# Value projections of a hybrid decoder block: 512 weight columns a matmul instead of 256

## What is computed

```
h = rmsnorm(x);  proj = h @ w_in          # w_in: 2048 x IN_COLS
nq, nkv, ngate, rq, rk, rv, rg, mq, bg = split(proj)
# nkv: (k_c, v_c, k_s, v_s, k_w, v_w), each 2 groups x 128 = 256 columns
# sparse attention: o = g0*softmax(q k_c')v_c' + g1*softmax(q k_s)v_s + g2*softmax(q k_w)v_w
#   k_c', v_c' = silu(blocks(k_c) @ cmp_w1) @ cmp_w2, and the same for v_c
# retention: 4 heads, rq, rk 128 columns each, rv 4 x 256 = 1024 columns
```

## Time and profile before

| | |
|---|---|
| median of 3 runs | 1707.71 us |
| profiled execution, its span from first to last instruction | 1705.8 us |
| PE busy | 1696.5 us (99%) |
| PE weight loads busy | 1468.2 us (86%) |
| DVE busy | 1132.7 us (66%) |
| ACT busy | 827.3 us (49%) |
| mean share of the 16 DMA engines on the main queue | 61.3% |
| DMA share in the v_s slot (251.2 to 266.6 us) | 0.88 |
| granted TensorE clock, mean | 0.999 |

### The profile page before, as it was taken

How to read it: one execution, slowest core, us unless ns; L and a number is a source line. 1 busy time by engine, 2 the same in 40 slices (tenths; PEclk the granted TensorE clock), 3 DMA queues, 4 the chain that set the end, 5 groups by cost and what they waited for, 6 DMA issues and landing times.

```text
span 1705.8 us, 25366 instructions
## 1 busy us (share of the span) xinstructions
PE 1696.5 (99%) x9082; PEld 1468.2 (86%) x9082; DVE 1132.7 (66%) x1522; ACT 827.3 (49%) x1139; POOL 48.0 (3%) x53
## 2 busy tenths in 40 slices
PE   9999999999999999999999999999999999999998
PEld 8888899999888888888888888888888888888886
DVE  7755676667475554554565777777776776776777
ACT  7544455444444444444444755455454555454453
POOL 1000000000140000000000000000000000000000
PEclk9999999999999999999999999999999999999999
DMA  9666478345656666666557566665666666656654
GB/s 304 189 230 198 138 232 260 118 142 159 202 158 185 197 190 194 212 195 196 188 186 242 177 188 197 193 199 185 195 190 189 186 192 189 190 191 192 193 176 148
DMA packets 245992, 327.78 MB, mean 192 GB/s; under 512 B 12907, under 2 KB 167308, under 8 KB 245388
## 3 DMA queue, kind: packets, MB, share of 16 engines
q1 hardware_dynamic: 245900, 326.47, 61.3%
HBM read 321.71 MB, written 3.67 MB: 191 GB/s over the span
## 4 chain that ended last, share of the span: by engine, by line
PE 98%; issue 1%; DVE 0%; DMA 0%; ACT 0%; POOL 0%; POOLq 0%; DVEq 0%; ACTq 0%
PE bank L1481 19%; PE bank L1471 15%; PE bank L1473 15%; PE bank L1472 15%; PE bank L1485 10%; PE bank L1494 7%; PE bank L1499 4%; PE bank L1458 1%; PE bank L1460 1%; PE bank L1459 1%; PE bank L1445 1%; PE bank L1447 1%; PE bank L1446 1%; PE bank L1766 0%; PE bank L1767 0%
## 5 line engine op out<-in xcount | busy, mean ns | idle before, releaser
L904 DVE TENSOR_TENSOR wlo<-wraw,whi 128x1024 fp32r<-128x1024 f32 x584 | 714.9, 1233 | 400.3 <-ACT whi L593 398.0
L593 ACT ACTIVATE whi<-wraw 128x1024 fp32r<-128x1024 f32 x584 | 616.7, 1059 | 625.2 <-PE bank L1473 378.7
L1481 PE MATMUL bank<-hx,whi 128*128 128x512 f32 x1376 | 344.5, 392 | 0.0
L1481 PEld LDWEIGHTS bank<-hx,whi 128*128 128x128 f32 x1376 | 248.0, 189 | 44.7
L1485 PEld LDWEIGHTS bank<-hx,wlo 128*128 128x128 f32 x1376 | 187.7, 190 | 13.4
L1485 PE MATMUL bank<-hx,wlo 128*128 128x256 f32 x1376 | 191.9, 282 | 0.0
L1471 PE MATMUL bank<-whi,hx 128*128 128x512 f32 x448 | 175.7, 392 | 0.0
L1473 PE MATMUL bank<-whi,hx 128*128 128x512 f32 x448 | 174.4, 389 | 0.0
L1472 PE MATMUL bank<-wlo,hx 128*128 128x512 f32 x448 | 174.3, 389 | 0.0
L1471 PE MATMUL bank<-whi,r_hi 128*128 128x512 f32 x384 | 149.8, 390 | 0.0
L1472 PE MATMUL bank<-wlo,r_hi 128*128 128x512 f32 x384 | 149.5, 389 | 0.0
(11 more groups left out here) (272 smaller groups left out, 2039.2 us busy)
## 6 DMA issues: line engine op xcount, KB each, us to landing
wraw<-in_w_in SPq DMA_DIRECT2D x200, 512.0 KB, 3.7
wraw<-in_w_up SPq DMA_DIRECT2D x176, 512.0 KB, 4.5
wraw<-in_w_down SPq DMA_DIRECT2D x88, 512.0 KB, 3.8
wraw<-in_w_mem_kv SPq DMA_DIRECT2D x32, 512.0 KB, 4.5
wraw<-in_w_o SPq DMA_DIRECT2D x32, 512.0 KB, 4.4
wraw<-in_w_br_mem SPq DMA_DIRECT2D x16, 512.0 KB, 4.4
wraw<-in_w_br_nsa SPq DMA_DIRECT2D x16, 512.0 KB, 4.3
wraw<-in_w_br_ret SPq DMA_DIRECT2D x16, 512.0 KB, 4.0
```

The lines of the kernel that those rows point to most:

```text
L593: nc.scalar.activation(whi[:, c], wraw[:, c], ACT.Copy).then_inc(hi_done, 1)
L904: V.tensor_tensor(wlo[:, c], wraw[:, c], whi[:, c].bitcast(F32), ALU.subtract).then_inc(lo_done, 1)
L1481: T.matmul(ps[UP_PAIRS[j][t]][:, :], whi[:, c, k, t * P:(t + 1) * P], hx[:, :, k0 + k, :], start=first and k == 0, stop=False, skip_group_ ...
```

## The change

- **Retention values.** The four quads of "rv" become two groups of two quads, each with 512 weight columns and 16 feature tiles. They use `chunk_w` (12 matmuls of 512 columns) in place of `chunk_n`. A group lives in two banks (0 and 7, then 1 and 0), and is read out once, by two DVE instructions of 128x512 at the end of its second quad. The loop over them is written out on PE and DVE.
- **Sparse values.** v_s and v_w are computed together: a matmul streams 256 columns of v_s from one buffer and 256 of v_w from another, 512 in all (`values_pair`). In quads 5 and 6, chunk 0 holds v_s and chunk 2 v_w of the same 4 feature tiles, and PE does both in 24 matmuls of 512 before the two compression chunks. In quad 9, chunks 0 and 1 are one pair and chunks 2 and 3 the next. `hidden` and `compressed` come in the middle of the two pairs. The sums stay in banks 1 and 4 from quad 5 to the end of quad 9, and are read out once.
- **Counting.** `values_pair` waits for the later of its two chunks and counts `pe_done` once it is through: in quads 5 and 6 by 1 after the pair and by 2 after the compression chunk 1; in quad 9 by 2 after each pair.
- The number of bytes loaded, of splits and of products is the same.

```diff
-          ("rqk", 4, 4), ("rv", 4, 4), ("rg", 4, 2),
+          ("rqk", 4, 4), ("rv", 4, 2), ("rg", 4, 2),
+RV_PAIRS = ((0, 7), (1, 0))
+VV_PAIR = (1, 4)
...
 # SP
-                         rows(w_in, 4 * (2 * h + c // 2), at))
-            quad(Q0["mix"] + 9, lambda c: rows(w_in, 4 * c, C_KV + 5 * GW))
-
-            loop(Q0["rqk"], 4, 2, cols(w_in, C_RQ))
+                         rows(w_in, 4 * h, C_KV + (3 + c) * GW) if n == 3 else rows(w_in, 4 * (2 * h + c // 2), at))
+            quad(Q0["mix"] + 9, lambda c: rows(w_in, 8 + 4 * (c // 2), (C_KV + 3 * GW, C_KV + 5 * GW)[c % 2]))
+
+            loop(Q0["rqk"], 2, 2, cols(w_in, C_RQ))
+            loop(Q0["rv"], 2, 2, wide_cols(w_in, C_RV), into_wide)
...
 # DVE
-                elif n == 3:
-                    by_row(q + 1, b, arena[:, A_VS:A_VS + 512], (), (), 3)
-                else:
+                elif n != 3:
...
-            by_row(q, 1, arena[:, A_VW:A_VW + 512], ())
+            dve.wait_ge(pe_done, 4 * q + 4)
+            for t in range(TT):
+                ch.add(V.tensor_scalar(arena[:, A_VS:A_VS + 2 * (A_VW - A_VS)].rearrange("p (a t n) -> p a t n", a=2, n=S)[:, :, t, :],
+                                       ps[VV_PAIR[t]][:, :].rearrange("p (a n) -> p a n", a=2), rstd_col(0, t), None, ALU.mult))
+            ch.wait()
+
+            dve.sem_inc(evac[1], 2)
+            ahead(q, (3,))
...
-                            by_row(q, j, arena[:, bass.ds(1024 * i + (base + 512 * j), 512)], ())
+                            if j:
+                                dve.wait_ge(pe_done, 4 * q + 4)
+                                for t in range(TT):
+                                    ch.add(V.tensor_scalar(by_head(A_RV + 1024 * i, t), ps[RV_PAIRS[i][t]][:, :].rearrange("p (h n) -> p h n", h=2),
+                                                           rstd_col(0, t), None, ALU.mult))
+                                ch.wait()
+                                dve.sem_inc(evac[i], 1)
+                            ahead(q, (3,))
...
 # PE
+            def values_pair(q, a, b, k0, first, last, between=None):
+
+                pe.wait_ge(lo_done, 4 * q + b + 1)
+                for t in range(TT):
+                    o = ps[VV_PAIR[t]][:, :]
+                    for k in range(CK):
+                        xh, xl = (v[:, k0 + k, t * P:(t + 1) * P] for v in (h_hi, h_lo))
+                        vh, vl = (v[:, a:b + 1:b - a, k, :] for v in (whi, wlo))
+                        T.matmul(o, xh, vh, start=first and k == 0, stop=False)
+                        T.matmul(o, xh, vl, start=False, stop=False)
+                        e = T.matmul(o, xl, vh, start=False, stop=last and k == CK - 1)
+                    if t == 0 and between is not None:
+                        between()
+                return e
...
-                    if n == 3:
-                        chunk_n(*at, b, *H, 4 * i, i == 0, i == 3)
-                    else:
+                    if n != 3:
                         chunk_d(*at, KEY_PAIRS[b], hx, 4 * i, i == 0, i == 3)
-                    compress_chunk(at[0], at[1] + 1, m, i)
-            quad(chunk_n, Q0["mix"] + 9, 1, (g + 5) // 2, H, {0: hidden, 2: compressed})
+                    elif i % 2 == 0:
+                        values_pair(at[0], 0, 2, 2 * i, i == 0, False).then_inc(pe_done, 1)
+                    compress_chunk(at[0], at[1] + 1, m, i, 2 if n == 3 and i % 2 == 0 else 1)
+            values_pair(Q0["mix"] + 9, 0, 1, 8, False, False, hidden).then_inc(pe_done, 2)
+            values_pair(Q0["mix"] + 9, 2, 3, 12, False, True, compressed).then_inc(pe_done, 2)
...
+            for i in range(2):
+                for j in range(2):
+                    scores, transposes, output = sparse(1, j, 2 * i + (HPG + j))
+                    scores()
+                    if j == 0:
+
+                        pe.wait_ge(evac[i], G0["rv"] // 2)
+                        if i:
+                            pe.wait_ge(evac[0], G0["rv"] // 2 + 1)
+                    for c in range(4):
+                        chunk_w(Q0["rv"] + 2 * i + j, c, RV_PAIRS[i], *H, 8 * j + 2 * c, j == 0 and c == 0, j == 1 and c == 3)
+                        if c == NSA_BEFORE[-1]:
+                            transposes()
+                    output()
```

More of the change, by code:

```diff
@@ L1105, in _, with sparse_softmax @@
                             ALU.mult).then_inc(s_kce, 1)
-            by_row(q, 1, arena[:, A_VW:A_VW + 512], ())
+            dve.wait_ge(pe_done, 4 * q + 4)
[5 more added lines that the diff above has]
+            ahead(q, (3,))
             dve.wait_ge(s_tab, 16)
             dve.wait_ge(s_sig, 1)
[L1111 to L1115, removed]
+            def sparse_softmax(g, i, j, h, q):
                         dve.wait_ge(a_s, h + 2)
@@ L1146, in _ @@
                         if g == 0:
-                            by_column(q, j, arena[:, bass.ds(1024 * i + (base + 512 * j), 512)], chunks=())
+                            by_column(q, j, arena[:, bass.ds(1024 * i + (A_RQ + 512 * j), 512)], chunks=())
                         else:
-                            by_row(q, j, arena[:, bass.ds(1024 * i + (base + 512 * j), 512)], ())
+                            if j:
[6 more added lines that the diff above has]
+                            ahead(q, (3,))
                         dve.wait_ge(a_h, h + 1)
@@ L1152, in _ @@
                                         ALU.subtract).then_inc(a_l, 1)
-                    ch.leave(2, NSA_LINKS * 2)
+            with dve.Fori(0, 2) as i:
+                ch.enter(i, NSA_LINKS * 2)
+                for j in range(2):
+                    sparse_softmax(0, i, j, 2 * i + j, 2 * i + (Q0["rqk"] + j))
+                ch.leave(2, NSA_LINKS * 2)
+            for i in range(2):
+                for j in range(2):
+                    sparse_softmax(1, i, j, 2 * i + (HPG + j), 2 * i + (Q0["rv"] + j))
             for i in range(2):
@@ L1756, in compressed, with compress_chunk @@
                 e.then_inc(s_kc, 1)
-            def compress_chunk(q, c, m, n):
+            def values_pair(q, a, b, k0, first, last, between=None):
[11 more added lines that the diff above has]
+                return e
+            def compress_chunk(q, c, m, n, done):
                 pe.wait_ge(s_bkl, m // 2 + 1)
@@ L1767, in compress_chunk @@
                     e = T.matmul(o, x_, wlo[:, c, k, :], start=False, stop=m % 2 == 1 and n == 3 and k == CK - 1)
-                e.then_inc(pe_done, 1)
+                e.then_inc(pe_done, done)
             g = G0["mix"]
@@ L1776, in _, with sparse @@
                     at = (q + i // 2, 2 * (i % 2))
-                    if n == 3:
-                        chunk_n(*at, b, *H, 4 * i, i == 0, i == 3)
-                    else:
+                    if n != 3:
                         chunk_d(*at, KEY_PAIRS[b], hx, 4 * i, i == 0, i == 3)
-                    compress_chunk(at[0], at[1] + 1, m, i)
-            quad(chunk_n, Q0["mix"] + 9, 1, (g + 5) // 2, H, {0: hidden, 2: compressed})
[L1785 to L1788, removed]
+                    elif i % 2 == 0:
[3 more added lines that the diff above has]
+            values_pair(Q0["mix"] + 9, 2, 3, 12, False, True, compressed).then_inc(pe_done, 2)
+            def sparse(g, j, h):
                         def scores():
@@ L1824, in output @@
                                      skip_group_check=True).then_inc(a_o, 1)
-                        quad((chunk_t, chunk_n)[g], q, j, i + G0[ph] // 2, H, {-1: scores, NSA_BEFORE[-1]: transposes, 3: output})
+                        return scores, transposes, output
+            with pe.Fori(0, 2) as i:
+                for j in range(2):
+                    scores, transposes, output = sparse(0, j, 2 * i + j)
+                    quad(chunk_t, 2 * i + (Q0["rqk"] + j), j, i + G0["rqk"] // 2, H, {-1: scores, NSA_BEFORE[-1]: transposes, 3: output})
+            for i in range(2):
+                for j in range(2):
+                    scores, transposes, output = sparse(1, j, 2 * i + (HPG + j))
[9 more added lines that the diff above has]
+                    output()
             octets("rg", H)
```

## The result

The changed kernel took 1718.25 us (median of 4 runs, 1716.53 to 1720.16), the kernel before 1707.6 us in the same comparison. The ratio is 1.0063, with a 95% interval of 1.0051 to 1.0075: 10.6 us slower. Forecast were 1715.5 us, a range of 1709.5 to 1719, and slower with a chance of 0.91.

The account below looks back on a forecast made before the run. PE's instruction stream was taken to bound the kernel. Waits of 3.84 + 3.2 + 3.1 and small terms of 0.4 make 10.5 us, less 2.7 for the stream: +7.8, so 1715.5 us; range for 8 in 10, 1709.5 to 1719.

Parts of the forecast that it names:

- signs that I had named for being wrong: In the trace after: PE starting the pair at once, a clock slice under 1.0, or a pair costing 0.24 us a matmul or more.
- Bound by PE's stream, waits not recovered: Whole kernel: PE is 99% busy, so any wait of PE lengthens the kernel by the full wait.
- Entry of quad 5: Before quad 5's pair: PE waits from 251.22 to 255.06 for the split of chunk (5, 2), +3.84 us.
- Quad 5 to quad 6: Before quad 6's pair: PE waits for rounding and three splits after the late release, +3.2 us (3.0 with overlapping splits, else 3.4).
- End of quad 9: Before head 0's scores: buffer 2 is released only when the last pair ends, so PE waits for `vc`, +3.1 us.
- Quad 9's start: Before quad 9's first pair: PE waits for the split of chunk (9, 1), +0.2 us.
- Stream: Fewer, wider matmuls: -1.7 us in "rv" after restart losses and -1.0 in "mix", together -2.7 us.
- "Hidden" work: Softmax, copies and read-out of two 512-column banks run beside other work and cost nothing.
- The clock: Rival: clock falls in PE's pauses, 2.6 us each; 1718.1 us after one fall, 1723.3 after three; chance 0.12. Forecast sum: nothing.

Follow-up runs that it names:

- e8: e3 with head 0's softmax maxima ahead of split 2 and the v_s/v_w read-out on DVE, split 3 after the probabilities: 1711.95 us.
- e6: e5 with quads 5 and 6 using chunks that hold both v_s and v_w, only quad 9 paired over two buffers, filling before head 0's scores: 1708.1 us.
- e5: Changed kernel plus ten spare 512-column matmuls before quad 5's pair, quad 6's pair and head 0's scores (the filled kernel): 1715.09 us.
- e1: Kernel before with only the retention values changed to 512 columns, sparse values as before: 1705.33 us.
- e3: e5 without the filling before head 0's scores, DVE making `kc` and `vc` before split 2 of the next quad: 1714.02 us.
- e2: Kernel before with only the sparse values paired, retention values as before: 1720.99 us.
- e7: e5 with each product of a pair done in two 256-column matmuls, one a buffer: 1715.24 us.
- e9: Changed kernel with v_s and v_w in one chunk in quads 5 and 6, quad 9 paired over two buffers, DVE's order of e8, no filling: 1705.48 us.

## Why the prediction was right, step by step

The mechanism and the sign were right, the total too small by 2.8 us. One of the signs that I had named for being wrong did appear: a slice of the clock under 1.0 (0.83 from 250 to 260 us), and with it a pair at 7.16 / 24 = 0.30 us a matmul. So the forecast's term for the clock, nothing, failed.

- **Bound by PE's stream, waits not recovered.** Right: each wait taken away came back in the total (e8: 1.8 expected, 2.1 measured; e6: 6.8 and 7.0, though its term for quad 9 is not borne out).
- **Entry of quad 5, +3.84.** 2.74 in the profile after, 3.0 in e5. The kind was right. The size was read from one execution in which the chain came late: DVE's read-out of quad 4 began at 252.34 there and at 251.11 after, 1.2 us earlier, with the same order of work up to that point. The trace of e1, whose mix phase is that of the kernel before, confirms it. Its rows (PE at the start of quad 5, then DVE's read-out of quad 4 and split (5, 2)):

```profile
250.97 0.28 PE L1473 MATMUL bank<-whi,hx 128*128 128x256 f32 x1
...
250.97 0.75 DVE L926 TENSOR_TENSOR arena<-bank,arena 128x256 f32<-128x256 f32 x2
...
252.63 1.23 DVE L907 TENSOR_TENSOR wlo<-wraw,whi 128x1024 fp32r<-128x1024 f32 x1 [0.18 <-ACT whi L596]
```

  There the split ended at 253.86, 2.9 us after PE came to the quad.
- **Quad 5 to quad 6, +3.2.** 2.99; the four splits took 4.63 us, so they overlap by 0.1 each, the lower of the two bounds.
- **End of quad 9, +3.1.** 3.14. But as a repair the step was incomplete: I named the read-out as "queued on DVE behind `vc`" with "only split 3" behind it. The head's softmax stands there as well, which e3 showed, once the wait ahead of it was gone.
- **Quad 9's start, +0.2.** 1.4: the term that was mis-sized most. I took the distance of split (9, 1) from PE as fixed. It was not: the data came late (ACT waited 1.51 us for them). Why they did stays open. With quads 5 and 6 as changed, the wait is 1.2 us in the trace after, 1.3 in e2, 1.0 in e5 and e8, 1.5 in e3 and none in e7. With their buffers released one by one it is 0.9 in e6 and none in e9.
- **Stream, -2.7.** In "rv" 2.2 where I had 1.7: a restart with 512 columns takes 2.83 us (408.09 - 405.26) and not 2.90, so the loss over 256 columns is 0.04, not 0.11. In the mix phase 0.7 where I had 1.0: each pair has a start-up of its own, 5.59 us instead of 24 x 0.2296 = 5.51 and 24 x 0.2267 = 5.44 later in a pair. Together 2.9.
- **"Hidden" work.** Right: e1 has no wait of PE in eight heads, with the read-out of two banks and all the softmax.
- **The clock.** It was left out of the sum and given 0.12 as a rival. It fell once in the profiled run, and the difference of the medians to e5 is 3.2 us. The median of 1718.25 lies at this rival's time for one fall, 1718.1. My argument against it, that the longest pause is shorter than the 5.2 us after which the clock fell at the end of the kernel, did not hold: it fell after 2.6. The price that I took from the first matmuls, 2.6 us, measured 1.6 in the short fall of the trace after and 2.8 in the long one of e2. Those rows were a poor source: the profile gives a granted clock of 1.00 over the first 9 us, and the same 20 matmuls last 7.30 us in the trace before and 6.34 in the one after. The Trainium skill ("TensorE: Matmul & The Clock Gate", "Why this matters for your kernels") warns of idle gaps between bursts of matmuls. The traces agree in the four pauses named above, and pauses of 2.8 and 3.0 us without a fall stand beside them.

Without the clock the forecast of 1715.5 would have met the filled kernel's 1715.09, but by luck: the entry wait was taken 1.1 too long and the one before quad 9 1.2 too short. The sum is better than its terms.

## What to carry to other kernels

Wider matmuls gain only a fixed cost each, here 13 ns; look first at what they need at once. Two buffers read by one instruction are wanted together and released together. Here the engines that refill them idled for 7 us through the pair and were waited for after it. Put what is read together into one buffer instead. When PE is the bound and a pause can't be avoided, count the clock with it, and look at everything queued on the engine that ends the pause: removing one entry brings up the next.

## What the runs showed of the hardware

- The granted clock fell to 0.50, 1.2 GHz, in or just after pauses of PE of 2.6 to 3.0 us, in some executions and not in others: in the profiled run of the changed kernel at one of the three, in that of e2 at all three. It stayed down for 3.4 us in three of these falls and for 6.8 us in the fourth, at a cost of 1.6 us (trace after, quad 5) and 2.8 us (e2, quad 6). With ten spare matmuls in each pause it stayed at 1.00 in the trace of e5. The changed kernel's runs spread over 3.6 us, the filled one's over 1.3.
- In the low stretch 512-column matmuls of a pair started 0.43 us apart (254.30 to 257.29 in the trace after, 7 intervals), at full clock 0.2267.
- A matmul that streams 2 x 256 columns out of two of the four weight buffers costs the same as one from a contiguous 512: 0.2267 us late in a pair.
- After a pause or small matmuls, most of what a stream of 512-column matmuls loses is in its first interval, 0.33 us in the rows of e5's pair (254.25 to 254.58); the next ones are 0.23.
